# Halving the first weight load, moving two weight splits, and feeding two chunks together in an attention layer

## The reference, cut to what matters

```python
y = swiglu(rms_norm(h, g[0]), w_gate, w_up, w_down);   h = h + 0.5 * rms_norm(y, g[1])
u = rms_norm(h, g[2])
y = mixer_ab(u, ...) if i % 2 == 0 else mixer_cd(u, ...)
h = h + rms_norm(y, g[3])
y = swiglu(rms_norm(h, g[4]), w_gate, w_up, w_down);   h = h + 0.5 * rms_norm(y, g[5])
```

## Time and profile before

| | |
|---|---|
| runs without a profile, median of 3 | 1182.44 us (1181.07 to 1182.83) |
| the profiled execution | 1181.1 us, span 1179.0 us |
| mean granted TensorE clock | 0.987 |
| PE busy | 1142.0 us, 97% of the span |
| DVE busy | 711.8 us, 60% |
| ACT busy | 545.3 us, 46% |
| read from HBM | 176.90 MB, 151 GB/s over the span |

### The profile page before, as it was taken

How to read it: one execution, slowest core, us unless ns; L and a number is a source line. 1 busy time by engine, 2 the same in 40 slices (tenths; PEclk the granted TensorE clock), 3 DMA queues, 4 the chain that set the end, 5 groups by cost and what they waited for, 6 DMA issues and landing times.

```text
span 1179.0 us, 19803 instructions
## 1 busy us (share of the span) xinstructions
PE 1142.0 (97%) x8837; PEld 1106.7 (94%) x8837; DVE 711.8 (60%) x746; ACT 545.3 (46%) x623; POOL 8.7 (1%) x12
## 2 busy tenths in 40 slices
PE   7999999999999899999999999999999799999998
PEld 7999999889999799999999999999899589999986
DVE  5665644668784676656546665644667727775642
ACT  5534343455643555344435534343454445544441
POOL 0000000000000000000000000000001100000000
PEclk9999999999999999999999999999999889999999
DMA  9456557676532145555454655556273014656550
GB/s 304 151 167 194 170 165 172 138 161 131 96 108 72 36 144 179 179 179 168 162 172 142 193 171 174 169 163 196 79 237 112 32 48 140 207 180 205 177 171 36
DMA packets 170291, 179.21 MB, mean 152 GB/s; under 512 B 4928, under 2 KB 163152, under 8 KB 170208
## 3 DMA queue, kind: packets, MB, share of 16 engines
q1 hardware_dynamic: 170208, 177.96, 50.2%
HBM read 176.90 MB, written 1.05 MB: 151 GB/s over the span
## 4 chain that ended last, share of the span: by engine, by line
PE 90%; DVE 5%; ACT 2%; DMA 2%; issue 1%; SPq 0%; DVEq 0%; ACTq 0%
PE ps L1617 23%; PE ps L1619 23%; PE ps L1618 23%; PE ps L1721 8%; PE ps L1688 2%; PE ps L1706 2%; PE ps L1705 2%; PE ps L1704 2%; PE ps L1654 2%; PE ps L1651 1%; PE ps L1655 1%; DMA raw<-ab_w_in 1%; DVE w_lo L1078 1%; DMA raw<-ffn_w_gate 1%; ACT u_hi L715 1%
## 5 line engine op out<-in xcount | busy, mean ns | idle before, releaser
L1617 PE MATMUL ps<-u_hi,w_hi 128*128 128x272 f32 (+1 forms) x1712 | 496.9, 290 | 2.9 <-DVE w_lo L1078 2.9
L1619 PE MATMUL ps<-u_hi,w_lo 128*128 128x272 f32 (+1 forms) x1712 | 493.2, 288 | 0.0
L1618 PE MATMUL ps<-u_lo,w_hi 128*128 128x272 f32 (+1 forms) x1712 | 491.2, 287 | 0.0
L1078 DVE TENSOR_TENSOR w_lo<-raw,w_hi 128x2048 fp32r<-128x2048 f32 (+1 forms) x168 | 375.8, 2259 | 127.3 <-ACT w_hi L659 127.2
L659 ACT ACTIVATE w_hi<-raw 128x2048 fp32r<-128x2048 f32 (+1 forms) x168 | 312.8, 1869 | 184.4 <-PE ps L1619 150.8
L1617 PEld LDWEIGHTS ps<-u_hi,w_hi 128*128 128x128 f32 x1712 | 323.2, 189 | 5.0 <-issue 3.5
L1618 PEld LDWEIGHTS ps<-u_lo,w_hi 128*128 128x128 f32 x1712 | 323.1, 189 | 0.3
L1619 PEld LDWEIGHTS ps<-u_hi,w_lo 128*128 128x128 f32 x1712 | 323.1, 189 | 0.0
L1617 PE MATMUL ps<-hid_hi,w_hi 128*128 128x272 f32 x528 | 152.2, 288 | 0.0
L1619 PE MATMUL ps<-hid_hi,w_lo 128*128 128x272 f32 x528 | 151.9, 288 | 0.0
L1618 PE MATMUL ps<-hid_lo,w_hi 128*128 128x272 f32 x528 | 151.8, 288 | 0.0
(11 more groups left out here) (320 smaller groups left out, 1107.6 us busy)
## 6 DMA issues: line engine op xcount, KB each, us to landing
raw<-ffn_w_gate SPq DMA_DIRECT2D x44, 1024.0 KB, 5.3
raw<-ffn_w_up SPq DMA_DIRECT2D x44, 1024.0 KB, 5.3
raw<-ffn_w_down SPq DMA_DIRECT2D x24, 896.0 KB, 4.9
raw<-ffn_w_down SPq DMA_DIRECT2D x20, 1024.0 KB, 5.1
raw<-ab_w_in SPq DMA_DIRECT2D x16, 1024.0 KB, 13.9
raw<-cd_w_in SPq DMA_DIRECT2D x9, 1024.0 KB, 5.4
raw<-ab_w_out SPq DMA_DIRECT2D x4, 1024.0 KB, 4.9
raw<-cd_w_out SPq DMA_DIRECT2D x4, 1024.0 KB, 4.9
```

The source lines that it names most:

```text
L1078: dve.tensor_tensor(dst, src, w_hi[:, n % NW, 0:rows(n) * CB].bitcast(F32), ALU.subtract)\
L1617: pe.matmul(o, wh, rhs_hi[:, kk, tok], start=first and kk == 0, stop=False)
L1618: pe.matmul(o, wh, rhs_lo[:, kk, tok], start=False, stop=False)
L1619: ins = pe.matmul(o, wl, rhs_hi[:, kk, tok], start=False, stop=last and kk == rows(n) - 1)
```

## The change

The first weight chunk is loaded by two transfers of four groups each, with a semaphore each. ACT starts its first split when the first has landed, and waits for the second at its second split. Chunk 2 is split (ACT and DVE) ahead of the squares of the first norm. For the ab sublayer the third chunk, b + 2, is no longer split ahead of the last output block of the first FFN, but behind the squares of the ab sublayer's first norm. In the cd sublayer `first_tiles` takes two chunks; the third goes to banks 4 and 5, `pre_norm_sum` follows the third chunk's first tile instead of the second's, and the pieces of stick-breaking stand one step later or so on all three engines.

```diff
+CD_BANK = (0, 2, 4, 0, 2, 0, 2, 0, 2)
...
+        s_rawa = sem("first_half_raw_loaded")
...
-                        load(b + 2 * j, wg[:, :, j * CB:(j + 1) * CB])
+                        if k == 0 and j == 0:
+                            for k0, done in ((0, s_rawa), (KD // 2, s_raw[0])):
+                                sp.dma_start(raw[:, 0, k0 * CB:(k0 + KD // 2) * CB].rearrange("p (k c) -> p k c", c=CB),
+                                             wg[:, k0:k0 + KD // 2, 0:CB]).then_inc(done, 16)
+                        else:
+                            load(b + 2 * j, wg[:, :, j * CB:(j + 1) * CB])
...
                     if k == 0 and g == 2:
+                        act.wait_ge(s_raw[0], 16)
...
                 if k == 0:
                     hi(1)
+                    hi(2)
                     square(0)
                     square(1)
                 square(2)
                 square(3)
-                if k == 0:
-                    hi(2)
+                if k == 1:
+                    hi(b + 2)
                 hi(b + 3)
...
                     if st > 1:
                         hi(b + st + 2)
-                    if st in (3, 5):
-                        stick_scores(st // 4)
-                    if st in (4, 6):
-                        act.activation(lb[st // 6][:, :, :], lb[st // 6][:, :, :], ACT.Ln, bias=1.0).then_inc(s_sp, 1)
-                    if st == 7:
+                    if st in (5, 6):
+                        act.activation(lb[st - 5][:, :, :], lb[st - 5][:, :, :], ACT.Ln, bias=1.0).then_inc(s_sp, 1)
+                    if st in (4, 5):
+                        stick_scores(st - 4)
+                    if st == 8:
                         stick_exp(0)
...
-            act.wait_ge(s_raw[0], 16)
+            act.wait_ge(s_rawa, 16)
...
                         for t in range(NT):
-                            hi(n + t + 3)
+                            if not (k == 0 and blk == NBLK - 1 and t == NT - 1):
+                                hi(n + t + 3)
...
                 if k == 0:
                     lo(1)
+                    lo(2)
...
                     dve.tensor_copy(convw[:, :], ps[:, 0, P:P + 4 * 12]).then_inc(s_cwc, 1)
-                    lo(2)
+                if k == 1:
+                    lo(b + 2)
                 lo(b + 3)
...
-                            lo(b + 2 * NPAIR + NT * blk + t + 3)
+                            if not (k == 0 and blk == NBLK - 1 and t == NT - 1):
+                                lo(b + 2 * NPAIR + NT * blk + t + 3)
...
-                    bank = 2 * ((st - 1) % 2)
+                    bank = CD_BANK[st - 1]
...
-                    if st == 4:
+                    if st == 5:
                         stick_log_beta(0)
-                    if st == 5:
+                    if st == 6:
                         stick_log_rest(0)
-                    if st == 6:
-                        stick_exponents(0)
                         stick_log_beta(1)
                     if st == 7:
                         stick_log_rest(1)
+                        stick_exponents(0)
...
-                    pe.wait_ge(s_cdc, 2 * x + 2)
+                    pe.wait_ge(s_cdc, x + 3)
...
-                for n in range(CD_CHUNKS):
-                    if n >= 2:
-                        pe.wait_ge(s_cdc, n - 1)
-                    if n == 0:
-                        first_tiles(k, b, 0, 1)
-                    else:
-                        tiles(b + n, 2 * (n % 2), u_hi, u_lo,
-                              between=(lambda: pre_norm_sum(k, "cd")) if n == 1 else None)
-                    if n in (2, 4):
-                        stick_scores(n // 4)
-                    if n == 5:
+                first_tiles(k, b, CD_BANK[0], 2)
+                for n in range(2, CD_CHUNKS):
+                    if n > 2:
+                        pe.wait_ge(s_cdc, n - 2 if n < 5 else n - 1)
+                    tiles(b + n, CD_BANK[n], u_hi, u_lo, between=(lambda: pre_norm_sum(k, "cd")) if n == 2 else None)
+                    if n in (3, 4):
+                        stick_scores(n - 3)
+                    if n == 6:
                         stick_sums(0)
```

## The result

The changed kernel is slower than the kernel before by 0.15%: ratio 1.0015, 95% interval 1.0009 to 1.0021 (medians of 20 runs each, 1183.35 and 1181.64 us). The forecast was 0.85 us faster; it is 1.7 slower. In absolute time it looks nearer, 1183.35 for a forecast of 1181.6, because the three runs that the forecast took as its base (1182.44) lay 0.8 us above the later median of the kernel before. The profiled execution has a span of 1181.5 us (1179.0 before) and a mean clock of 0.985 (0.987).

What follows compares the result with a forecast made beforehand. PE was taken to bound the kernel, busy 97% of the span. Start -5.0, FFN to ab -1.5 and cd +5.65 summed to -0.85 us, 1181.6 us on the median of 1182.44; range 1178.2 to 1184.7.

Steps and rivals of the forecast that it cites:

- Part 1: At the start, split first load and earlier split of chunk 2 let PE start chunks 1 and 2 sooner: -5.0 us.
- the rival of a half that lands with the whole: At the start, the first half-load lands only with the whole: start gains 3.5, total +0.65, 1183.1 us; chance 0.12.
- Part 2: First FFN to ab sublayer: 2.25 us won at the FFN's end, 0.7 lost before the third chunk: -1.5 us.
- Part 3: The cd sublayer: two chunks together gain 2.6 us, waits for the third copy and `lm` and low clock cost more: +5.65.
- The rivals without the first stall: In cd, load of b + 5 sooner or DVE ahead, so both stalls go: -9.1 us, 1173.3 us; chance 0.07.
- with half of it: In cd, first stall comes without lower clock, ACT and DVE catch up before the sums: -3.95, 1178.5 us; chance 0.13.
- the lower clock behind the first stall: In cd, behind the wait for the third copy, one stretch at the lower clock: 1.3 us (ends 0 and 4.3).
- two chunks together: In cd, first two chunks end 15.02 us behind `lnv`, at 854.18 against 856.76 one by one: -2.6 us.
- stall in front of the scores, with its restart: In cd, PE waits for DVE's copy of the third chunk before the first scores: 4.9 us, restart 0.25.
- wait for `lm`, with its restart: In cd, `stick_sums(0)` waits 1.55 us for DVE's `lm`, restart 0.25: +1.8 us (0 to 3).
- The slower rival: In cd, clock stays down behind the new stalls: both, total +6.5, 1188.9 us; first alone +2.15, 1184.6; chance 0.08.
- Its case of one stretch: In cd, clock stays low for 9.5 us behind the first stall alone: total +2.15, 1184.6 us; chance 0.02.

Runs made afterwards that it cites:

- Part 1 alone: Kernel before with only the first chunk loaded in two transfers and chunk 2 split ahead of the squares: 0.9959, -4.8 us.
- Experiment 3: Changed kernel, two versions: load of chunk b + 5 ahead of the seven tables, 0.9945; DVE's third copy ahead of `lo(b + 5)`, 0.9996; ratios to before.
- experiment 6: Changed kernel with first four heads' `lm` one step earlier on DVE: 0.9935 with chunk b + 5's load ahead of the tables, 0.9933 with the third copy first.
- experiment 4: Changed kernel with 18 unused matmuls in front of the first scores: 0.9983 with full rows, 0.9980 with half the rows, against before.
- the order alone: Kernel before with only chunk 2 split ahead of the squares, first load in one piece: 0.9987, 1.5 us faster.
- the load first with `lm` earlier: Changed kernel with chunk b + 5's load ahead of the tables and first four heads' `lm` one step earlier on DVE: 0.9935 to before, 1172.96 us.
- both versions with the copy first: Changed kernel with DVE's third copy ahead of `lo(b + 5)`: 0.9996, 1181.61 us; the same with `lm` one step earlier: 0.9933, 1172.68 us.
- parts 1 and 2 alone: Kernel before with the start's and the ab sublayer's changes, without the cd sublayer's: 0.9946, -6.4 us.
- part 3: As a run: kernel before with only the cd sublayer's changes (two chunks fed together): 1.0085, +10.0 us.
- part 3 again: Kernel before with only the cd sublayer's changes, run a second time: 1.0077, +9.1 us.
- parts 1 and 3: Kernel before with the start's and the cd sublayer's changes, without the ab sublayer's: 1.0037, +4.4 us.

## Why the prediction was wrong

- **Part 1, forecast -5.0: right.** Part 1 alone measured -4.8. Starts of chunk 1 and 2 were forecast at 18.89 and 25.8, and came at 19.14 and 25.95. The first half landed at 9.6 and not at 9.37; the rival of a half that lands with the whole falls.
- **Part 2, forecast -1.5: right.** `lnv` of the ab sublayer came 7.10 sooner, 2.24 more than that of the first norm (forecast 2.25), the third chunk was late by 0.46 (forecast 0.45).
- **Part 3, mechanism right.** The two chunks ended 15.02 us behind `lnv`, as forecast, the scores waited 4.5 us (forecast 4.9) for the third copy, and the sums 1.6 (forecast 1.55) for `lm`. Experiment 3 shows the load and the copy behind it as the cause of the first, experiment 6 DVE's order as that of the second. The rivals without the first stall, and with half of it, fall.
- **The term that failed: the lower clock behind the first stall.** It was set at 1.3 us, from the stretch at 29.5, and measured 3.6 (experiment 4; the scores 2.4 and chunk 4 1.2 of it in the trace). The row chosen was one with dense matmuls behind 2.6 us of idle time. Here the idle time was longer and the scores came behind it. The bound of 4.3 had held it, but neither the value nor the chances leaned towards it. The terms of part 3 up to window attention, from `lnv`:

| term | forecast, us | traces, us |
|---|---|---|
| two chunks together | -2.6 | -2.6 |
| stall in front of the scores, with its restart | 4.9 + 0.25 | 4.5 |
| lower clock behind it | 1.3 | 3.6 |
| wait for `lm`, with its restart | 1.8 | 1.9 |
| sum | 5.65 | 7.35 |

- **A second term, put at nothing: window attention.** "Window attention follows PE as before" stood for 0, and it took 1.5 us more in the trace. With it part 3 comes to 8.85. With -4.86 and -1.58 for parts 1 and 2 the changed kernel's trace is 2.4 us longer than that of before, 3.3 more than forecast: the lower clock is 2.3 of it and window attention 1.5, and the stall was 0.6 cheaper. By the medians of the runs the miss is 2.55.
- **Where those 1.5 us come from** is shown in part. From its start to the `lnv` behind it window attention took 71.5 to 71.7 us in seven traces, 70.3 to 70.6 in eight, and 70.0, 70.2 and 68.7 in before, the order alone and the load first with `lm` earlier. That order follows the clock: each trace has a wait of 2.28 us for `probs` there, and the lower level ended 13.9 to 14.2 us behind that wait in the seven, 11.6 to 12.3 in the eight, and 11.1, 11.6 and 6.6 in the three. But the seven hold all five traces of part 3 as it was and also both versions with the copy first, which have no stall in front of the scores. What shifts the clock there is open, and so is whether part 3 costs this 1.5 us in every execution.
- The slower rival (the clock stays down behind the stalls) named what happened. It asked for 9.5 us behind each of two stalls; the first had 7.6 and the second none. Its case of one stretch, +2.15 us, came nearest to the measured +1.7. It deserved more than 0.08, and the forecast's own value should have moved towards it.

## What to carry to other kernels

Feeding two chunks together moved the norm's sum 3.45 us later, and a load hung on that sum for no reason of data. When a step moves, look for what is listed behind its waits on every queue, SyncE's too, and follow it to the next engine that waits. Price a stall of PE twice: its length, and the slow work behind it, by what comes next; here 4.5 us of idle time in front of sparse matmuls cost 3.6 more. Cured of its two waits (one line on SyncE, one on DVE), the same change is 0.65% faster than the kernel before. That it is also faster than parts 1 and 2 alone is likely from the 2.61 us that its traces save ahead of window attention; the times can't tell it (0.9935, 0.9921 to 0.9949, against 0.9946, 0.9933 to 0.9958).

## What the runs showed of the hardware that was not expected

- Unused matmuls in place of a stall of 4.5 us made the kernel 3.7 to 4.0 us faster, with all 128 rows or with 64. Activity on half the rows kept the clock at the full level.
- The clock does not fall at a fixed point of an idle time. Behind 2.2, 2.3 and 2.4 us of it at the end of the first FFN it fell in three traces (order alone, part 1, part 3), behind 2.28, 2.7 and 2.2 us at the same place in three others (before, part 3 again, parts 1 and 3) it did not; and in three of seven traces of the stall of 4.5 to 4.8 us it fell only when PE had resumed work.
- The Trainium skill, "TensorE: Matmul & The Clock Gate" (What's actually happening), says that activity releases a throttle that is on by default. The traces agree: behind each stall of 4.5 to 4.8 us the full level came back 3.7 to 8.0 us into PE's work. They suggest that not all activity releases it alike: with scores that filled PE for 4.1 to 5.2 us at the lower level it came back only in chunk 4 behind them (five traces), with dense matmuls within 3.7 and 4.4 us (two traces).
- With a wait of 2.6 us in front of the sums twelve runs of one kernel differ by 10 us (mean clocks 0.980 to 0.989); without it five runs differ by 3.7.
